# GpSimd's element-wise operations in gate, up and the MLP's entry as two pieces of 256 columns

## What is computed

```python
hn = rms_norm(h, norm2_g)
gate, up = jnp.split(hn @ w_gate_up, 2, axis=-1)      # D_FF = 2816
return h + (jax.nn.silu(gate) * up) @ w_down
```

## Time and profile before

| | us |
|---|---|
| median of 3 executions | 2211.3 (2209.63 to 2213.07) |
| the profiled execution's own time | 2210.53 |
| its span in the profile | 2208.8 |
| TensorE busy in the span | 2155.6 (98%) |
| VectorE busy | 1428.3 (65%) |
| GpSimd busy | 1066.1 (48%) |

### The profile page before, as it was taken

One profiled execution on the slowest core, in us unless ns is written; L12 is line 12 of the kernel. 1 busy time (PEld: TensorE's weight loads), 2 busy tenths in 40 slices (PEclk: granted clock), 3 DMA queues, 4 the chain that ended last, 5 costly groups with the idle time before them and its releaser, 6 DMA issues.

```text
span 2208.8 us, 30063 instructions
## 1 busy us (share of the span) xinstructions
PE 2155.6 (98%) x10720; PEld 1779.9 (81%) x10720; DVE 1428.3 (65%) x2807; ACT 917.8 (42%) x1628; POOL 1066.1 (48%) x759
## 2 busy tenths in 40 slices
PE   7999999999999999999999999999999999999998
PEld 6986788998888787887777788888888878888976
DVE  5278799999952567743697666656467736206934
ACT  6244522332225675533443323323456454226832
POOL 1365433556454334247676455555498623132173
PEclk9999999999999999999999999999999999999999
DMA  3412211111224213135525454445966331111131
GB/s 117 132 49 72 66 49 48 48 49 43 62 86 135 78 49 101 44 126 181 171 77 180 148 181 139 151 149 191 340 214 200 106 115 48 48 48 39 51 113 77
DMA packets 244855, 238.74 MB, mean 108 GB/s; under 512 B 10849, under 2 KB 187134, under 8 KB 244718
## 3 DMA queue, kind: packets, MB, share of 16 engines
q1 hardware_dynamic: 240560, 223.76, 31.4%
q10 hardware_dynamic: 4158, 13.16, 1.5%
HBM read 174.54 MB, written 61.15 MB: 107 GB/s over the span
## 4 chain that ended last, share of the span: by engine, by line
PE 82%; DVE 8%; POOL 3%; issue 3%; ACT 3%; DMA 1%; SPq 0%; ACTq 0%; DVEq 0%; POOLq 0%
PE ps L1014 29%; PE ps L1335 14%; PE ps L1363 9%; PE ps L1409 9%; PE ps L1207 6%; PE ps L1630 3%; PE ps L1180 2%; PE ps L1246 2%; DVE score L2483 1%; PE ps L1229 1%; PE ps L1074 1%; PE ps L1608 1%; DMA wdr<-in_w_down 1%; PE ps L1112 1%; POOL wr_lo L3374 1%
## 5 line engine op out<-in xcount | busy, mean ns | idle before, releaser
L3206 POOL TENSOR_TENSOR w_lo<-w_raw,w_hi 128x256 fp32r<-128x256 f32 (+2 forms) x241 | 303.0, 1278 | 572.6 <-ACT w_hi L1659 572.6
L1014 PE MATMUL ps<-x_hi,w_hi 128*128 128x512 f32 (+2 forms) x960 | 360.7, 376 | 0.6 <-ACT mix_s L1800 0.4
L1014 PE MATMUL ps<-x_lo,w_hi 128*128 128x512 f32 (+2 forms) x960 | 358.4, 373 | 0.0
L1014 PE MATMUL ps<-x_hi,w_lo 128*128 128x512 f32 (+2 forms) x960 | 356.5, 371 | 0.0
L1014 PEld LDWEIGHTS ps<-x_hi,w_hi 128*128 128x128 f32 x960 | 180.4, 188 | 37.2 <-issue 4.8
L1014 PEld LDWEIGHTS ps<-x_hi,w_lo 128*128 128x128 f32 x960 | 180.6, 188 | 28.7
L1014 PEld LDWEIGHTS ps<-x_lo,w_hi 128*128 128x128 f32 x960 | 180.1, 188 | 28.6 <-issue 0.2
L2514 DVE MATCH_REPLACE8 score<-best,score 128x400 f32<-128x400 f32 (+3 forms) x224 | 185.3, 830 | 0.0
L2510 DVE MAX8 best<-score 128x8 f32<-128x400 f32 (+3 forms) x224 | 181.4, 844 | 1.4
L1659 ACT CAST w_hi<-w_raw 128x1024 fp32r<-128x1024 f32 (+1 forms) x129 | 127.8, 990 | 104.1 <-PE ps L1014 69.6
L1335 PE MATMUL ps<-x_hi,wr_hi 128*128 128x512 f32 x352 | 140.0, 398 | 5.4 <-DVE a L2861 2.2
(11 more groups left out here) (480 smaller groups left out, 5364.2 us busy)
## 6 DMA issues: line engine op xcount, KB each, us to landing
w_raw<-in_w_in SPq DMA_DIRECT2D x74, 512.0 KB, 3.8
wdr<-as_scratch SPq DMA_DIRECT2D x77, 256.0 KB, 3.6
rawg<-in_w_gate_up SPq DMA_DIRECT2D x22, 512.0 KB, 4.0
rawu<-in_w_gate_up SPq DMA_DIRECT2D x22, 512.0 KB, 5.3
wdr<-in_w_down SPq DMA_DIRECT2D x22, 512.0 KB, 6.6
as_scratch<-ac SPq DMA_DIRECT2D x44, 256.0 KB, 3.7
wt_scratch<-wdr SPq DMA_DIRECT2D x33, 256.0 KB, 4.7
as_scratch<-a SPq DMA_DIRECT2D x33, 256.0 KB, 3.7
```

Of the source, the lines that this page charges most:

```text
L1014: mm = pe.matmul(ps[:, b, 0:n], w[:, s, P * k:P * k + P], r[:, k, t0:t0 + n], start=k == 0 and i == 0, stop=k == kd - 1 and i == 2 and ext ...
L3206: low = pool.tensor_tensor(w_lo[:, p % 2, a:a + step], w_raw[:, p % 2, a:a + step], w_hi[:, p % 2, a:a + step], ALU.subtract)
```

## The change

GpSimd's `tensor_tensor` of 128x512 becomes two of 128x256, one on columns 0 to 255 and one on columns 256 to 511, in `block_low`, `x_low`, `down_combined` and the products of halves. The semaphore is counted up by the second piece alone, so everything that waited for the whole operation waits for both pieces. The order of the work, the data and the waits stay. `inner_low`, `normed_low`, `with_residual` and `final_sums` stay whole, and so do all of VectorE's operations.

```diff
+            def in_halves(out_, a, b, op):
+
+                for o in (slice(0, BANK // 2), slice(BANK // 2, BANK)):
+                    half_ = pool.tensor_tensor(out_[:, o], a[:, o], b[:, o], op)
+                return half_
...
-                pool.tensor_tensor(wr_lo[:, q % SLOTS, :], block_source(q), wr_hi[:, q % SLOTS, :], ALU.subtract).then_inc(wl_even, 1)
+                in_halves(wr_lo[:, q % SLOTS, :], block_source(q), wr_hi[:, q % SLOTS, :], ALU.subtract).then_inc(wl_even, 1)
...
-                pool.tensor_tensor(xb(1, prod, k), x_source(y), xb(0, prod, k), ALU.subtract).then_inc(xl_even, 1)
+                in_halves(xb(1, prod, k), x_source(y), xb(0, prod, k), ALU.subtract).then_inc(xl_even, 1)
...
-                pool.tensor_tensor(wt1[:, :], wdr[:, 1, :], wdr[:, 0, :], ALU.subtract).then_inc(wdt_done, 1)
+                in_halves(wt1[:, :], wdr[:, 1, :], wdr[:, 0, :], ALU.subtract).then_inc(wdt_done, 1)
                 pool.wait_ge(wdt_done, WDT_DONE_0 + 4 * j + 1)
-                pool.tensor_tensor(wdr[:, 1, :], wdr[:, 3, :], wdr[:, 1, :], ALU.subtract).then_inc(wdt_done, 1)
+                in_halves(wdr[:, 1, :], wdr[:, 3, :], wdr[:, 1, :], ALU.subtract).then_inc(wdt_done, 1)
...
-                        pool.tensor_tensor(a[1][:, :], a[1][:, :], g1[0][:, :], ALU.mult).then_inc(am_done, 1)
+                        in_halves(a[1][:, :], a[1][:, :], g1[0][:, :], ALU.mult).then_inc(am_done, 1)
...
-                        pool.tensor_tensor(a[0][:, :], a[0][:, :], g0[0][:, :], ALU.mult).then_inc(am_done, 1)
+                        in_halves(a[0][:, :], a[0][:, :], g0[0][:, :], ALU.mult).then_inc(am_done, 1)
```

More of the change, by code:

```diff
@@ L3409, in down_combined @@
                 pool.wait_ge(wd_load, WD_LOAD_0 + 32 * j + 32)
-                pool.tensor_tensor(wt1[:, :], wdr[:, 1, :], wdr[:, 0, :], ALU.subtract).then_inc(wdt_done, 1)
+                in_halves(wt1[:, :], wdr[:, 1, :], wdr[:, 0, :], ALU.subtract).then_inc(wdt_done, 1)
                 pool.wait_ge(wdt_done, WDT_DONE_0 + 4 * j + 1)
-                pool.tensor_tensor(wdr[:, 1, :], wdr[:, 3, :], wdr[:, 1, :], ALU.subtract).then_inc(wdt_done, 1)
+                in_halves(wdr[:, 1, :], wdr[:, 3, :], wdr[:, 1, :], ALU.subtract).then_inc(wdt_done, 1)
                 pool.wait_ge(wdt_done, WDT_DONE_0 + 4 * j + 2)
-                pool.tensor_tensor(wdr[:, 0, :], wdr[:, 1, :], wdr[:, 0, :], ALU.add).then_inc(wdt_done, 1)
+                in_halves(wdr[:, 0, :], wdr[:, 1, :], wdr[:, 0, :], ALU.add).then_inc(wdt_done, 1)
                 pool.wait_ge(wdt_done, WDT_DONE_0 + 4 * j + 3)
-                pool.tensor_tensor(wdr[:, 2, :], wdr[:, 2, :], wdr[:, 0, :], ALU.subtract).then_inc(wdt_done, 1)
+                in_halves(wdr[:, 2, :], wdr[:, 2, :], wdr[:, 0, :], ALU.subtract).then_inc(wdt_done, 1)
             block_low(6)
@@ L3429, in _ @@
                 pool.wait_ge(sil_done, silu(n, 1))
-                pool.tensor_tensor(a_st[0][n][1][:, :], a_st[0][n][1][:, :], g1[n][:, :], ALU.mult).then_inc(am_done, 1)
+                in_halves(a_st[0][n][1][:, :], a_st[0][n][1][:, :], g1[n][:, :], ALU.mult).then_inc(am_done, 1)
                 if n == 0:
@@ L3434, in _ @@
                 pool.wait_ge(po_done, po(n, 5))
-                pool.tensor_tensor(a_st[0][n][0][:, :], a_st[0][n][0][:, :], g0[n][:, :], ALU.mult).then_inc(am_done, 1)
+                in_halves(a_st[0][n][0][:, :], a_st[0][n][0][:, :], g0[n][:, :], ALU.mult).then_inc(am_done, 1)
             for n in range(2, FC):
```

## The result

The changed kernel is **slower by 0.8%**: its median is 2227.9 us (2225.65 to 2230.21, 4 runs), that of the kernel before beside it 2210.5 us (4 runs), the ratio 1.0083 with a 95% interval of [1.0068, 1.0097] (ratios below are given in the same way). The profiled execution took 2227.28 us, 16.7 us more than the one before. Forecast were 2221.4 us (2210 to 2229) and "slower" with 0.74. So the sign and, in gate and up, the mechanism came out, and the size was 6.5 us short.

A forecast was written before the change was run, and what follows sets the result against it. The bound was taken as TensorE plus a chain through GpSimd, loads and VectorE in each pair of steps. Pairs +12.4, steps 2 and 3 -1.8, entry queue -0.5 gave +10.1 us: median 2221.4 us, range 2210 to 2229.

The forecast's parts named there:

- The chain and its anchor: Gate and up, per pair of steps: TensorE's P1, GpSimd's low part, SyncE's loads, DMA, seven GpSimd operations, VectorE, P7; +1.6 us.
- the low part that yields to L2664: GpSimd's low part that SyncE's loads wait for lets VectorE's L2664 pass between its pieces: +0.6 us per pair; anchor.
- the seven operations: GpSimd's operations from L3410 to the low part ahead of VectorE's sums, each 0.14 us longer: +1.0 us per pair.
- VectorE's four sums: From GpSimd's last low part to L2861's end, smaller pieces but two more collisions: -0.2 us per pair.
- The DMA: w_down's loads later and stores of inner sums earlier, so more overlap: +0.2 us per pair, between nothing and 0.8.
- The pairs' sum: Chain's +1.6 us paid eight times, steps 5 to 19, less 0.4 for step 13's slack: +12.4 us (7.6 to 17.2).
- rival 3: TensorE's clock drops behind each of the eight longer waits in gate and up: +10.4 us more, 2232 us; chance 0.07.
- steps 2 and 3: VectorE's sums collide with shorter pieces, taking away TensorE's waits of 0.9 and 0.8 us: -1.8 us (0 to -2).
- VectorE's row: Entry's VectorE queue up to 1138 us, most gains given back by a second collision: -0.5 us (0 to -2).
- rival 4: GpSimd gets into VectorE's entry queue at 1123, eight pieces costing 0.55 us each: +4.4 us, 2225.8 us; chance 0.13.
- Rival 1: Faster, as the lock is held half as long and TensorE waited for VectorE: 2206.8 us; chance 0.11.
- Rival 2: No change, as the chain in gate and up has more give than one step shows: 2211.8 us; chance 0.14.

The follow-up runs named there:

- moved sums: VectorE's sums for the next step moved behind L2861, in both kernels: 2208.2 us with whole operations, 2207.1 us with halves.
- both edits: Changed kernel with L2861 ahead of combined_weights and block_low(14) ahead of down_combined(0): 2203.6 us, ratio 0.9973; the same with whole operations 2208.1 us.
- re-ordered entry: Changed kernel with block_low(14) put ahead of the first down_combined in GpSimd's order: 2224.4 us, ratio 1.0072.
- the kernel with the memset: Kernel before, whole operations, with one 0.2 us memset of an unused tile ahead of GpSimd's first L3410: 2208.5 us, ratio 0.9996.

## Why the prediction was right, and where it was short

- **The chain and its anchor: right.** Each link is there in gate and up, +0.59 us for the low part that yields to L2664 (0.6 forecast), +1.05 for the seven operations (1.0), -0.26 for VectorE's four sums (-0.2). The moved sums show that the loss of the eight pairs hangs on this chain alone.
- **The DMA: mis-sized.** +0.47 us instead of +0.2, 2 us over eight pairs. The prediction had the stores 0.5 us earlier and the loads 0.6 later, 1.1 us more overlap; measured are 5.38 and 3.33 us from loads to stores, 2.05 us. VectorE's last store operand, L2840, took 1.785 us on average before, colliding each time, and 0.69 after. Choosing a value "nearer nothing, since the bytes are the same" was the slip: the bytes are the same, but only the loads are on the chain. It was inside the bounds (0 to 0.8), and holding the stores back took 0.9 us off this link. That the overlap grows with the stores' nearness is only part of it: at 4.83 us the link was as long as at 3.33.
- **The pairs' sum: 12.4 us forecast, 14.5 measured**, the DMA's 2 us.
- **The clock (rival 3, 0.07): paid once, not eight times.** Behind the longest gap, in step 15, eight matmuls ran at half rate (granted clock 0.50, the level of 1.2 GHz), +1.55 us. First the timeline there, then the busy times by stretch, ahead of the granted clock, the DMA's share and GB/s; the second stretch lies behind step 13's gap of 2.47 us, which cost nothing:

```profile
1424.74 0.47 PE L1335 MATMUL ps<-x_hi,wr_hi 128*128 128x512 f32 x1 [2.56 <-DVE a L2861]
...
1425.94 0.63 PE L1335 MATMUL ps<-x_lo,wr_hi 128*128 128x512 f32 x1
```

```profile
1425.50:1428.50 3.00, 3.00 (x9) 2.31 (x8) 0.00 (x0) 0.00 (x0) 1.18 (x2) 0.50 1.02 302
...
1383.00:1386.00 3.00, 3.00 (x14) 2.43 (x15) 0.40 (x2) 0.35 (x1) 1.44 (x2) 1.00 0.87 258
```

- **The entry: wrong in sum.** Forecast were -1.8 us for steps 2 and 3 and -0.5 for VectorE's row. The first came out: the waits of 1.0 and 0.9 us (by the starts) are gone. But rival 4 (0.13) came true beside the forecast instead of in its place (timeline: GpSimd, then VectorE's row):

```profile
1121.32 2.41 POOL L3373 TENSOR_TENSOR wt<-wdr 128x256 f32<-128x256 f32 x2 [2.89 <-DMA wdr<-in_w_down]
1123.81 6.77 POOL L3373 TENSOR_TENSOR wdr<-wdr 128x256 f32<-128x256 f32 x6
```

```profile
1120.71 3.57 DVE L2685 TENSOR_TENSOR xl_P<-mix,xh_P 128x512 fp32r<-128x512 f32 x4
1124.20 4.66 DVE L2769 TENSOR_TENSOR mix<-mix 128x512 f32<-128x512 f32 x4
```

  Eight pieces each lengthened one of VectorE's operations by about 0.55 us, as rival 4 priced it (two in the first of these rows, four in the second, and the two L2672 behind them, 1.21 us each), and the wait behind that row grew to 3.79 us, with seven slow matmuls behind it. A wait of 1.25 us for block 14's low part is new as well, where the prediction had no added wait. By the starts of the same matmuls the changed kernel is 1.45 us ahead at the last one ahead of gate and up's first block (1093.84 against 1095.29 us), and 0.39 us ahead at the last one before step 5's P7 (1216.31 against 1216.70): **+1.1 us where -2.3 was forecast**, the largest of the misses. Rivals had been weighed as alternatives; this one could be added to the forecast, and its 4.4 us would have made 2225.8.
- **The down projection: right**, nothing. From P7 of step 20 to 1743 us the distance to the kernel before stays at 15.71 us.
- **GpSimd's busy time: +53 us instead of +30.** The 211 x 0.14 us left out the second yield of each operation that meets VectorE. The pieces' true price is higher still, since the 13.87 us for which the first L3410 stood had counted as busy and fell to 2.41. In gate and up it cost nothing outside the chain, as the kernels with moved sums show.
- **Rival 1 (faster)** failed in this kernel: TensorE waited for VectorE, but VectorE for GpSimd. A gain of the size that it gave appears only with both edits. **Rival 2** fell with the first link: the chain had no give.

Sum: 14.5 + 1.55 + 1.1 = 17.15 us, where the distance between the two executions goes from -1.45 us ahead of the entry to +15.7 behind gate and up. Against the 10.1 us forecast, 3.4 are missing in the entry, 2.1 in the pairs and 1.55 in the clock. That the span differs by nearly the same, 16.7 us, is partly luck: the changed kernel's execution came to the entry 1.45 us earlier and lost 1.0 us behind the down projection. No edit touches either stretch, and the other executions differ there as well (461.7 to 465.4 us from the 132 matmuls at 1670 us to the 288 at 2134).

The rule that was weighed here (the Trainium skill, SBUF — State Buffer, "Who interferes with whom": the later instruction of two is blocked until the first has finished) agrees with every collision of VectorE's sums in gate and up after the change, 1.01 to 1.23 us for a sum behind a piece of 0.7. It disagrees with the 13.87 us of the earlier trace rows and the 13.50 us above, in which some twenty operations of VectorE passed one of GpSimd.

## What to carry to other kernels

Splitting an operation halves what the other engine waits, and doubles the number of times that its own engine yields: the low part here went from 1.64 to 2.22 us where VectorE had an operation waiting, and from 1.29 to 1.44 us where it had none. So ask of each operation whether the chain that ends last runs through the one who waits or through the one who yields; here first moving L2861 ahead of work that waited for GpSimd made the loss of 0.8% vanish, and the entry's re-ordering on top of it a gain of 0.3%. And where loads on the chain share their queues with stores that are not on it, price how much sooner the stores come, not only how much later the loads do. Last, ask of each rival whether it could come true beside the forecast and not in its place.

## What the runs showed of the hardware

- GpSimd can be passed over for a whole row of VectorE's operations that follow each other without a gap (13.87 us, again 13.50 and 13.86 us), and can also get in behind the one that runs (1121.32, 1124.41 us). Neither the piece's size nor a shift of 0.37 us in the time of asking explains it.
- A gap in TensorE's work is followed by matmuls at the lower clock only at times. Behind gaps of 2.73 us (step 15) and 3.95 us (entry) seven or eight ran at half rate; behind 2.47 and 2.26 us none, and none behind 2.65 us with `block_low` alone in pieces, though in the kernel with the re-ordered entry eight did behind 2.20 us. In the earlier trace rows the wait of 2.8 us was followed by seven slow ones, while the kernel with the memset had the same wait, 2.81 us, and none behind it. What tips it can't be read from these rows.
- Holding seven stores back took 0.9 us off loads of 9.7 us in the changed kernel, and 0.2 us off 9.25 us where the stores had started 2 us later.
